# Attention over paired heads: row and column halves of TensorE side by side, scores two pairs ahead, values in parts behind the transposes

## The chip, the cores and the metric

The kernel runs on one core of a Trainium2 chip. The metric is the device time of one execution in microseconds (us); lower is better. Times are the median of several executions.

## The reference, cut to what matters

The program is a network of two blocks over 256 latent tokens (and, in the first block, 256 context tokens) of width 1024. The first block has two layers, each with a feed-forward part, a mixer and a second feed-forward part. The change touches the attention inside the mixer alone. Eight heads of 64 channels; a latent query sees a window of latent keys with a relative bias (others masked) and all 256 context keys; in layer 0 the context tokens also attend to themselves.

```python
def context_attention(q, k, v):
    s = jnp.einsum('bqhd,bkhd->bhqk', q, k, preferred_element_type=jnp.float32) * (NA_HEAD_DIM ** -0.5)
    p = jax.nn.softmax(s, axis=-1).astype(v.dtype)
    return jnp.einsum('bhqk,bkhd->bqhd', p, v).reshape(B, L, NA_CH)

# neighbourhood_attention, per row of the grid
s_loc = einsum(q_r, k_b) * scale + bias
s_ctx = einsum(q_r, k_ctx) * scale
p = softmax(concatenate([s_loc, s_ctx], axis=-1))
o = einsum(p_loc, v_b) + einsum(p_ctx, v_ctx)
```

## The kernel before, in words

Each engine runs its own list of instructions, written out by hand, and waits on counting semaphores. The program is a row of stages. The one of interest is class `Mix`; ahead of it stands `MixIn` (the projection, which fills `u` with queries and keys, channels on the partitions, and `v` with values, tokens on the partitions), behind it `AddProduct` (the output projection, which reads `y`). `Mix` appears once in each layer. In layer 0 it handles two groups: g=0, the latent queries against 512 keys (256 latent, 256 context), and g=1, the context queries against 256 keys. In layer 1 there is only g=0.

An item w is 128 queries (tile `qt`) of one head `h` of one group. There are 8 x 2 items a group. Each passes through this chain:

- **scores** (TensorE, L1267): a product that contracts the 64 channels of a head. Even heads lie on partitions 0 to 63, odd heads on 64 to 127, so the product uses one row half of the array (`po`). It writes 128 x 512 (or 256) into bank w % 2. It waits until VectorE has read item w-2 (`scores_read`).
- **scale** (VectorE, L1367, L1368 and L1371, L1374): scale and bias into `sc`, a ring of four, then the negated row maximum. It waits for the scores, and for the transposes of item w-4, which read the same slot.
- **exps** (ScalarE, L1319): exponential with row sum.
- **normalise** (VectorE, L1382, L1383): reciprocal of the sum, and the product with it.
- **transposes** (TensorE, L1277): one a key tile of 128, four with 512 keys, two with 256, into bank 2 + w % 2.
- **copies** (ScalarE, L1329): from the bank into `pt`, the transposed probabilities.
- **values** (TensorE, L1289): for a whole head (two items), one product a key tile, 128 x 64 weights, 256 columns, summed in one column half of bank 4 or 5.
- **move** (ScalarE, L1337): that half of the bank into `y`, 64 partitions at a time.

TensorE's order is: scores of items 0 to 2; then for each w the scores of w+3, the transposes of w, and on every even w from 2 on the values of the head before. VectorE's order is scale(w+2), normalise(w). ScalarE's is exps(w+2), copies(w), and a move every second item. GpSimd computes the convolution and pooling mixers at the same time (`mixed`); at the end TensorE runs the pooling product (L1307), ScalarE copies it (L1351) and the next stage rounds `y` into operands (L1423, L1435) before its first product (L255).

Of the kernel before, what the change touches and what calls it, by code (L numbers as in the profile page):

```python
# [25 lines left out]
P = 128  # L26
D = 1024
KT = D // P
S = 256
# [21 lines left out]
NA_H, DH = 8, 64  # L51
# [338 lines left out]
A_POOL = A_PT + 2048  # L390
# [802 lines left out]
class Mix:  # L1193
    def __init__(self, chip, layer, last, mix_in):
# [3 lines left out]
        self.sc, self.pt = chip.part(A_SC, 4, 512), chip.part(A_PT, 2, 4, S)  # L1198
# [7 lines left out]
        self.items = [(g, h, qt) for g in range(ng) for h in range(NA_H) for qt in range(2)]  # L1206
# [3 lines left out]
        self.product, self.moved, self.mixed = chip.product.take(n // 2 + 1), chip.moved.take(n // 2), chip.mixed.take(1)  # L1210
        self.y_there = chip.y_there.take(2)

    def keys(self, g):
        return (0, T2) if g == 0 else (S, T2)

# [40 lines left out]
    def tensor(self, pe):  # L1256
# [4 lines left out]
        def scores(w):  # L1261
            g, h, qt = items[w]
            lo, hi = keys(g)
            po, q0 = 64 * (h % 2), g * S + qt * P
            if w >= 2:
                pe.wait_ge(self.scores_read.sem, self.scores_read.at(w - 1))
            nc.tensor.matmul(chip.bank[w % 2][:, 0:hi - lo], u[po:po + 64, CH_Q + h // 2, q0:q0 + P],  # L1267
                             u[po:po + 64, CH_K + h // 2, lo:hi], start=True, stop=True)\
                .then_inc(self.scored.sem, 1)
# [11 lines left out]
        def values(n):  # L1281
            g, h, _ = items[2 * n]
            po = 64 * (h % 2)
            pe.wait_ge(self.copied.sem, self.copied.at(2 * n + 2))
            if n >= 2:
                pe.wait_ge(self.moved.sem, self.moved.at(n - 1))
            nkt = (keys(g)[1] - keys(g)[0]) // P
            for kt in range(nkt):
                mm = nc.tensor.matmul(chip.bank[4 + n % 2][po:po + 64, 0:S],  # L1289
                                      v[:, kt + 4 - nkt, h * DH:(h + 1) * DH], pt[:, n % 2, kt, :],  # L1290
                                      start=(kt == 0), stop=(kt == nkt - 1))
            mm.then_inc(self.product.sem, 1)
# [18 lines left out]
    def scalar(self, act):  # L1311
# [10 lines left out]
        def copies(w):  # L1322
            g, h, qt = items[w]
            nkt = (keys(g)[1] - keys(g)[0]) // P
            n = w // 2
# [3 lines left out]
            nc.scalar.activation(pt[:, n % 2, 0:nkt, qt * P:(qt + 1) * P],  # L1329
                                 chip.bank[2 + w % 2][:, 0:nkt * P].rearrange("p (k q) -> p k q", q=P), ACT.Copy)\  # L1330
                .then_inc(self.copied.sem, 1)

        def move(n):
            g, h, _ = items[2 * n]
            po = 64 * (h % 2)
            act.wait_ge(self.product.sem, self.product.at(n + 1))
            nc.scalar.activation(y[po:po + 64, 4 + h // 2, g * S:(g + 1) * S], chip.bank[4 + n % 2][po:po + 64, 0:S],  # L1337
# [4 lines left out]
        for w in range(len(items)):  # L1342
# [3 lines left out]
            if w >= 3 and w % 2 == 1:  # L1346
                move(w // 2 - 1)
        move(len(items) // 2 - 1)
        act.wait_ge(self.product.sem, self.product.at(len(items) // 2 + 1))
# [4 lines left out]
    def vector(self, dve):  # L1354
# [3 lines left out]
        def scale(w):  # L1358
            g, h, qt = items[w]
            n = keys(g)[1] - keys(g)[0]  # L1360
            s, bank = sc[:, w % 4, :], chip.bank[w % 2]
# [1153 lines left out]
```

## Time and profile before

| | us |
|---|---|
| median of 3 runs | 3099.96 (3099.4 to 3101.96) |
| the profiled execution's own time | 3101.26 |
| its span | 3099.5 |
| TensorE busy (matmul) | 2884.9 (93%) |
| VectorE busy | 2186.3 (71%) |
| ScalarE busy | 1235.7 (40%) |
| `Mix` in layer 0, scores of item 0 to pooling product | 78.9 |
| `Mix` in layer 1, the same | 51.7 |

### The profile page before, as it was taken

Reading aid. Unit: us, or ns where it says so; the run is one execution under the profiler, and the core shown is the slowest. Engines: PE = TensorE matmul, PEld = TensorE weight load, DVE = VectorE, ACT = ScalarE, POOL = GpSimd, SP = SyncE. Lnnn points to the kernel's source line nnn. Section 1 sums busy time; section 2 is a strip of 40 time slices with the busy share of each in tenths; the row PEclk is TensorE's granted clock in tenths of the full one; section 3 lists DMA queues with packets and bytes.
Section 4 is the critical chain, followed back from the end, with each engine's and each line's share of the span. In section 5 each row is a group of like instructions: output and inputs, shape, how many; then the busy total and the mean of one; then the engine's idle time right before and its main releaser. Section 6 shows DMA issues by size and latency. Waiting matters only on the chain. (4 is left out here: it accounts for less than half of the span.)

```text
span 3099.5 us, 46116 instructions
## 1 busy us (share of the span) xinstructions
PE 2884.9 (93%) x15682; PEld 2422.1 (78%) x15682; DVE 2186.3 (71%) x4187; ACT 1235.7 (40%) x2282; POOL 369.4 (12%) x413
## 2 busy tenths in 40 slices
PE   7999999999999999999999997596479999999997
PEld 4888878567888778887859996376368999999997
DVE  2999994559898975657466664365997777777775
ACT  2323243443232332224354453153125555444554
POOL 0111116001111100100400000000473000000000
PEclk9999999999999999999999998798559999999999
DMA  5555443133545444544415556023003655666563
GB/s 233 177 176 203 170 142 102 34 109 136 197 173 194 178 162 143 185 142 148 130 49 170 180 175 216 0 69 109 1 0 96 188 185 187 186 186 188 184 189 115
DMA packets 107703, 449.94 MB, mean 145 GB/s; under 512 B 11952, under 2 KB 12592, under 8 KB 94256
## 3 DMA queue, kind: packets, MB, share of 16 engines
q1 hardware_dynamic: 93744, 347.46, 35.2%
q0 software_dynamic: 13824, 100.67, 8.6%
q8 instruction: 86, 1.41, 0.2%
q14 instruction: 49, 0.40, 0.0%
HBM read 447.04 MB, written 1.05 MB: 145 GB/s over the span
## 5 line engine op out<-in xcount | busy, mean ns | idle before, releaser
L178 DVE TENSOR_TENSOR weight_lo<-weight_ring,weight_hi 128x512 fp32r<-128x512 f32 x1272 | 945.5, 749 | 530.8 <-ACT weight_hi L171 515.8
L171 ACT ACTIVATE weight_hi<-weight_ring 128x512 fp32r<-128x512 f32 x1272 | 800.8, 632 | 1164.4 <-PE bank L257 1163.5
L255 PE MATMUL bank<-operand_hi,weight_hi 128*128 128x256 f32 (+1 forms) x3168 | 1039.4, 328 | 24.0 <-DVE operand_lo L592 13.0
L256 PE MATMUL bank<-operand_lo,weight_hi 128*128 128x256 f32 (+1 forms) x3168 | 1034.7, 327 | 0.0
L257 PE MATMUL bank<-operand_hi,weight_lo 128*128 128x256 f32 (+1 forms) x3168 | 1034.5, 327 | 0.0
L255 PEld LDWEIGHTS bank<-operand_hi,weight_hi 128*128 128x128 f32 x3168 | 603.7, 191 | 91.8 <-issue 21.4
L256 PEld LDWEIGHTS bank<-operand_lo,weight_hi 128*128 128x128 f32 x3168 | 603.9, 191 | 54.6
L257 PEld LDWEIGHTS bank<-operand_hi,weight_lo 128*128 128x128 f32 x3168 | 603.8, 191 | 50.8
L850 DVE SCALAR_TENSOR_TENSOR extension_ffn<-extension_ffn,silu_c 128x512 f32<-128x512 f32 x532 | 388.7, 780 | 1.7
L255 PE MATMUL bank<-hidden_hi_ffn,weight_hi 128*128 128x512 f32 (+1 forms) x704 | 256.6, 364 | 4.0 <-DVE arena L1095 4.0
L256 PE MATMUL bank<-hidden_lo_ffn,weight_hi 128*128 128x512 f32 (+1 forms) x704 | 255.3, 363 | 0.0
L257 PE MATMUL bank<-hidden_hi_ffn,weight_lo 128*128 128x512 f32 (+1 forms) x704 | 255.3, 363 | 0.0
L255 PE MATMUL bank<-weight_hi,act_hi_experts 128*128 128x512 f32 x512 | 201.0, 393 | 1.0 <-DVE act_lo_experts L265 1.0
L256 PE MATMUL bank<-weight_lo,act_hi_experts 128*128 128x512 f32 x512 | 200.7, 392 | 0.0
L257 PE MATMUL bank<-weight_hi,act_lo_experts 128*128 128x512 f32 x512 | 199.2, 389 | 0.0
L255 PEld LDWEIGHTS bank<-hidden_hi_ffn,weight_hi 128*128 128x128 f32 x704 | 132.9, 189 | 28.5 <-DVE arena L1095 6.7
L817 POOL TENSOR_TENSOR mod_lo_ffn<-extension_ffn,mod_hi_ffn 128x1024 fp32r<-128x1024 f32 (+1 forms) x44 | 98.3, 2233 | 427.9 <-ACT mod_hi_ffn L859 427.9
L257 PEld LDWEIGHTS bank<-hidden_hi_ffn,weight_lo 128*128 128x128 f32 x704 | 132.9, 189 | 20.8
L256 PEld LDWEIGHTS bank<-hidden_lo_ffn,weight_hi 128*128 128x128 f32 x704 | 132.9, 189 | 20.5
L801 POOL DMA_DIRECT2D extension_ffn<-in_w_mods x88 | 53.7, 613 | 716.5 <-DVE extension_ffn L850 590.9
L2026 POOL TENSOR_SCALAR arena<-iota,arena 128x128 f32<-128x128 f32 x192 | 125.6, 672 | 78.0 <-ACT arena L2127 78.0
L2142 PE MATMUL bank<-arena 128*128 128x128 f32 x512 | 122.6, 401 | 6.8 <-DVE arena L2038 5.2
(260 smaller groups left out, 2740.1 us busy)
## 6 DMA issues: line engine op xcount, KB each, us to landing
weight_ring<-in_ffn SPq DMA_DIRECT2D x272, 512.0 KB, 3.6
weight_ring<-in_experts SPq DMA_DIRECT2D x256, 512.0 KB, 3.6
extension_ffn<-in_w_mods POOLq DMA_DIRECT2D x96, 1024.0 KB, 7.5
weight_ring<-in_w_mix SPq DMA_DIRECT2D x56, 512.0 KB, 3.6
weight_ring<-in_w_second SPq DMA_DIRECT2D x52, 512.0 KB, 4.0
extension_mixer<-in_rel_bias SPq DMA_DIRECT2D x2, 1536.0 KB, 6.8
arena<-in_x SPq DMA_DIRECT2D x1, 2048.0 KB, 9.4
arena<-in_cmp_k SPq DMA_DIRECT2D x1, 2048.0 KB, 11.8
```

The costliest lines, as they stand in the source:

```text
L171: nc.scalar.activation(self.hi[:, g % 2, h], self.ring[:, g % NS, h], ACT.Copy).then_inc(self.rounded, 1)
L178: self.nc.vector.tensor_tensor(self.lo[:, g % 2, h], self.ring[:, g % NS, h], self.hi[:, g % 2, h].bitcast(F32), ALU.subtract).then_inc(se ...
L255: nc.tensor.matmul(out, a_hi, b_hi, start=start and n == 0, stop=False)
L256: nc.tensor.matmul(out, a_hi, b_lo, start=False, stop=False)
L257: last = nc.tensor.matmul(out, a_lo, b_hi, start=False, stop=stop and n == len(pairs) - 1)
L801: pool.dma_start(self.w[:, j, u, :, :], src).then_inc(self.loaded[j].sem, 16)
L817: nc.gpsimd.tensor_tensor(self.lo[:, 0:n], self.flat(j), self.hi[:, 0:n].bitcast(F32), ALU.subtract)\
L850: ins = nc.vector.scalar_tensor_tensor(acc, w, scale, acc, ALU.mult, ALU.add)
L2026: nc.gpsimd.tensor_scalar(b[:, t % HOTS, :], iota[:, :], columns[:, 1, t:t + 1], None, ALU.is_equal)\
L2142: nc.tensor.matmul(chip.bank[4 + j // 2][:, (j % 2) * P:(j % 2 + 1) * P], a[:, j, :], b[:, j, :], start=True, stop=True).then_inc(chip.spr ...
```

## The change

Heads are handled in pairs. The items of a pair are two neighbouring heads with the same query tile, so that even w is the lower row half and odd w the upper.

- Scores: both products of a pair are issued back to back, into two banks of a ring of four (0, 1, 6, 7 instead of 0, 1). Pair n waits until VectorE has read pair n-2. Pairs 0 and 1 are issued ahead; pair 1 after `MixIn`'s last evictions, since it uses banks 6 and 7. The pair w/2 + 2 is issued before the transposes of even w.
- Values: four items (two heads, two query tiles) make one group n. A part is one key tile: two products back to back, the two heads in the two column halves of one bank. Part w % 4 of group w/4 - 1 follows the transposes of item w, for w from 4 on. The last group's parts stand after the loop.
- `pt` is twice as large (8 x 512 words): [key tile][head of the pair, query]. The copies write it at another place, with the same shape.
- Moves: one for both heads, 128 partitions, half as many; each is issued later.

VectorE's order and instructions stay, but for the bank that scale reads.

```diff
-        self.sc, self.pt = chip.part(A_SC, 4, 512), chip.part(A_PT, 2, 4, S)
+        self.sc, self.pt = chip.part(A_SC, 4, 512), chip.part(A_PT, 8, 4 * P)
...
-        self.items = [(g, h, qt) for g in range(ng) for h in range(NA_H) for qt in range(2)]
+        self.items = [(g, 2 * hp + j, qt) for g in range(ng) for hp in range(NA_H // 2) for qt in range(2) for j in range(2)]
...
+    def score_bank(self, w):
+        return (0, 1, 6, 7)[w % 4]
+
+    def turned_probs(self, n, j, kt):
+
+        return self.pt[:, 4 * (n % 2) + kt, :].rearrange("p (j q) -> p j q", j=2)[:, j, :]
...
+        def scores(n):
+            if n >= 2:
+                pe.wait_ge(self.scores_read.sem, self.scores_read.at(2 * n - 2))
+            for w in (2 * n, 2 * n + 1):
+                g, h, qt = items[w]
+                lo, hi = keys(g)
+                po, q0 = 64 * (h % 2), g * S + qt * P
+                nc.tensor.matmul(chip.bank[self.score_bank(w)][:, 0:hi - lo], u[po:po + 64, CH_Q + h // 2, q0:q0 + P],
+                                 u[po:po + 64, CH_K + h // 2, lo:hi], start=True, stop=True)\
+                    .then_inc(self.scored.sem, 1)
...
+        def values(n, part):
+
+            g, _, _ = items[4 * n]
             nkt = (keys(g)[1] - keys(g)[0]) // P
+            if part >= nkt:
+                return
+            if part == 0:
+                pe.wait_ge(self.copied.sem, self.copied.at(4 * n + 4))
+                if n >= 2:
+                    pe.wait_ge(self.moved.sem, self.moved.at(n - 1))
+            for j in range(2):
+                h = items[4 * n + j][1]
+                mm = nc.tensor.matmul(chip.bank[4 + n % 2][64 * j:64 * j + 64, 0:S],
+                                      v[:, part + 4 - nkt, h * DH:(h + 1) * DH], self.turned_probs(n, j, part),
+                                      start=(part == 0), stop=(part == nkt - 1))
+            if part == nkt - 1:
+                mm.then_inc(self.product.sem, 1)
...
-        for w in range(3):
-            scores(w)
+        scores(0)
         pe.wait_ge(evicted.sem, evicted.at(20))
+        scores(1)
         for w in range(len(items)):
-            if w + 3 < len(items):
-                scores(w + 3)
+            if w % 2 == 0 and w // 2 + 2 < len(items) // 2:
+                scores(w // 2 + 2)
             transposes(w)
-            if w >= 2 and w % 2 == 0:
-                values(w // 2 - 1)
-        values(len(items) // 2 - 1)
+            if w >= 4:
+                values(w // 4 - 1, w % 4)
+        for part in range(4):
+            values(len(items) // 4 - 1, part)
...
-            if w >= 3 and w % 2 == 1:
-                move(w // 2 - 1)
-        move(len(items) // 2 - 1)
+            if w >= 8 and w % 4 == 1:
+                move(w // 4 - 2)
+        move(len(items) // 4 - 2)
+        move(len(items) // 4 - 1)
```

Here is TensorE's order at the start of the stage in layer 0, before. L1267 are scores, L1277 transposes, L1289 values; x4 counts calls in a row.

```order
L1267 MATMUL bank<-extension_mixer 128x512 x4
L1277 MATMUL bank<-ident,extension_mixer 128x128 x4
L1267 MATMUL bank<-extension_mixer 128x512
L1277 MATMUL bank<-ident,extension_mixer 128x128 x4
L1267 MATMUL bank<-extension_mixer 128x512
L1277 MATMUL bank<-ident,extension_mixer 128x128 x4
L1289 MATMUL bank<-extension_mixer 64x256 x4
```

The same place with the change (scores L1275, transposes L1285, values L1301).

```order
L1275 MATMUL bank<-extension_mixer 128x512 x6
L1285 MATMUL bank<-ident,extension_mixer 128x128 x8
L1275 MATMUL bank<-extension_mixer 128x512 x2
L1285 MATMUL bank<-ident,extension_mixer 128x128 x8
L1275 MATMUL bank<-extension_mixer 128x512 x2
L1285 MATMUL bank<-ident,extension_mixer 128x128 x4
L1301 MATMUL bank<-extension_mixer 64x256 x2
L1285 MATMUL bank<-ident,extension_mixer 128x128 x4
L1301 MATMUL bank<-extension_mixer 64x256 x2
```

Six scores stand ahead of the first transposes instead of four, the first values stand behind the fifth item's transposes instead of the third's, and they come two products at a time, one in each column half.

The end of the stage in layer 1, TensorE, before:

```order
L1277 MATMUL bank<-ident,extension_mixer 128x128 x8
L1289 MATMUL bank<-extension_mixer 64x256 x4
L1277 MATMUL bank<-ident,extension_mixer 128x128 x4
L1289 MATMUL bank<-extension_mixer 64x256 x4
L1307 MATMUL bank<-arena,pool_w_pooling 128x256 x2
```

And with the change:

```order
L1285 MATMUL bank<-ident,extension_mixer 128x128 x4
L1301 MATMUL bank<-extension_mixer 64x256 x2
L1285 MATMUL bank<-ident,extension_mixer 128x128 x4
L1301 MATMUL bank<-extension_mixer 64x256 x10
L1321 MATMUL bank<-arena,pool_w_pooling 128x256 x2
```

Behind the last transposes stand ten value products instead of four: one part of the group before, and all four parts of the last group.

## Rows read from the trace of the kernel before

**Rows 1.** Windows: start:end, length, busy of PE, PEld, DVE, ACT, POOL; clock, DMA share, GB/s.

```profile
563.60:570.00 6.40, 4.33 (x10) 1.36 (x10) 5.46 (x13) 6.10 (x12) 0.00 (x0) 0.91 0.21 83
570.00:579.00 9.00, 9.00 (x21) 4.21 (x22) 5.74 (x15) 4.01 (x11) 0.00 (x0) 0.50 0.00 0
579.00:642.60 63.60, 57.20 (x230) 27.54 (x228) 40.28 (x118) 35.38 (x96) 0.00 (x0) 1.00 0.00 1
...
1549.40:1555.50 6.10, 4.18 (x9) 1.24 (x8) 5.21 (x12) 5.85 (x11) 0.00 (x0) 0.98 0.27 86
1555.50:1565.50 10.00, 9.85 (x23) 4.67 (x24) 5.99 (x16) 4.26 (x11) 0.00 (x0) 0.50 0.00 0
1565.50:1601.10 35.60, 32.06 (x131) 15.60 (x129) 20.64 (x54) 18.15 (x40) 0.00 (x0) 1.00 0.00 1
```

**Rows 2.** Timeline, two items with 512 keys: start us, duration us, engine, instruction.

```profile
585.63 1.12 PE L1267 MATMUL bank<-extension_mixer 64*128 64x512 f32 x2
586.69 0.66 PE L1277 MATMUL bank<-ident,extension_mixer 128*128 128x128 f32 x4
...
588.19 0.15 DVE L1382 RECIPROCAL rsum<-rsum 128x1 f32<-128x1 f32 x1
...
588.92 0.66 PE L1277 MATMUL bank<-ident,extension_mixer 128*128 128x128 f32 x4 [0.52 <-DVE extension_mixer L1383]
...
589.50 1.94 PE L1289 MATMUL bank<-extension_mixer 128*64 128x256 f32 x8
...
590.16 0.15 DVE L1382 RECIPROCAL rsum<-rsum 128x1 f32<-128x1 f32 x1
...
591.37 1.12 PE L1267 MATMUL bank<-extension_mixer 64*128 64x512 f32 x2
```

**Rows 3.** Timeline, two items with 256 keys.

```profile
621.18 0.70 PE L1267 MATMUL bank<-extension_mixer 64*128 64x256 f32 x2
621.81 0.44 PE L1277 MATMUL bank<-ident,extension_mixer 128*128 128x128 f32 x2
622.18 0.70 PE L1267 MATMUL bank<-extension_mixer 64*128 64x256 f32 x2
622.71 0.15 DVE L1382 RECIPROCAL rsum<-rsum 128x1 f32<-128x1 f32 x1
...
623.68 1.08 PE L1289 MATMUL bank<-extension_mixer 128*64 128x256 f32 x4
623.96 0.15 DVE L1382 RECIPROCAL rsum<-rsum 128x1 f32<-128x1 f32 x1
...
624.68 0.70 PE L1267 MATMUL bank<-extension_mixer 64*128 64x256 f32 x2
```

**Rows 4.** Timeline, start of the stage in layer 0.

```profile
563.63 1.98 PE L1267 MATMUL bank<-extension_mixer 64*128 64x512 f32 x4
...
569.90 1.11 PE L1277 MATMUL bank<-ident,extension_mixer 128*128 128x128 f32 x4 [1.51 <-DVE extension_mixer L1383]
...
571.33 0.49 DVE L1383 TENSOR_SCALAR extension_mixer<-extension_mixer,rsum 128x512 f32<-128x512 f32 x1
...
573.99 2.07 PE L1267 MATMUL bank<-extension_mixer 64*128 64x512 f32 x2
575.99 1.11 PE L1277 MATMUL bank<-ident,extension_mixer 128*128 128x128 f32 x4
...
577.04 2.93 PE L1289 MATMUL bank<-extension_mixer 128*64 128x256 f32 x8
```

**Rows 5.** Timeline, TensorE at the end of the stage in both layers.

```profile
642.53 1.98 PE L1307 MATMUL bank<-arena,pool_w_pooling 128*128 128x512 f32 x4
...
1597.90 0.66 PE L1277 MATMUL bank<-ident,extension_mixer 128*128 128x128 f32 x4
1599.24 1.94 PE L1289 MATMUL bank<-extension_mixer 128*64 128x256 f32 x8 [0.69 <-ACT extension_mixer L1329]
1601.12 1.13 PE L1307 MATMUL bank<-arena,pool_w_pooling 128*128 128x256 f32 x4
```

More of the change, by code:

```diff
@@ L389 @@
 A_PT = A_SC + 2048
-A_POOL = A_PT + 2048
+A_POOL = A_PT + 4096
 A_MIXER = A_POOL + 2048 - A_WORDS
@@ L1209, in __init__ @@
             s.take(n) for s in (chip.scored, chip.scores_read, chip.maxed, chip.exped, chip.probs, chip.turned, chip.copied))
-        self.product, self.moved, self.mixed = chip.product.take(n // 2 + 1), chip.moved.take(n // 2), chip.mixed.take(1)
+        self.product, self.moved, self.mixed = chip.product.take(n // 4 + 1), chip.moved.take(n // 4), chip.mixed.take(1)
         self.y_there = chip.y_there.take(2)
@@ L1259, in tensor @@
         evicted = self.mix_in.evicted
[L1261 to L1269, printed above, removed]
+        def scores(n):
[8 more added lines that the diff above has]
+                    .then_inc(self.scored.sem, 1)
         def transposes(w):
@@ L1324, in copies @@
             nkt = (keys(g)[1] - keys(g)[0]) // P
-            n = w // 2
+            n = w // 4
             act.wait_ge(self.turned.sem, self.turned.at(w + 1))
@@ L1328, in copies @@
                 act.wait_ge(self.product.sem, self.product.at(n - 1))
-            nc.scalar.activation(pt[:, n % 2, 0:nkt, qt * P:(qt + 1) * P],
+            at = S * (w % 2) + P * qt
+            nc.scalar.activation(pt[:, 4 * (n % 2):4 * (n % 2) + nkt, at:at + P],
                                  chip.bank[2 + w % 2][:, 0:nkt * P].rearrange("p (k q) -> p k q", q=P), ACT.Copy)\
@@ L1333, in move @@
         def move(n):
-            g, h, _ = items[2 * n]
-            po = 64 * (h % 2)
+            g, h, _ = items[4 * n]
             act.wait_ge(self.product.sem, self.product.at(n + 1))
-            nc.scalar.activation(y[po:po + 64, 4 + h // 2, g * S:(g + 1) * S], chip.bank[4 + n % 2][po:po + 64, 0:S],
+            nc.scalar.activation(y[:, 4 + h // 2, g * S:(g + 1) * S], chip.bank[4 + n % 2][:, 0:S],
                                  ACT.Copy).then_inc(self.moved.sem, 1)
@@ L1345, in scalar @@
             copies(w)
-            if w >= 3 and w % 2 == 1:
-                move(w // 2 - 1)
-        move(len(items) // 2 - 1)
-        act.wait_ge(self.product.sem, self.product.at(len(items) // 2 + 1))
+            if w >= 8 and w % 4 == 1:
+                move(w // 4 - 2)
+        move(len(items) // 4 - 2)
+        move(len(items) // 4 - 1)
+        act.wait_ge(self.product.sem, self.product.at(len(items) // 4 + 1))
         for b in range(2):
@@ L1360, in scale @@
             n = keys(g)[1] - keys(g)[0]
-            s, bank = sc[:, w % 4, :], chip.bank[w % 2]
+            s, bank = sc[:, w % 4, :], chip.bank[self.score_bank(w)]
             dve.wait_ge(self.scored.sem, self.scored.at(w + 1))
```

11 lines of the change are left out of this document (removed).

## The prediction

> **What bounds the kernel now.** I read three views of the one profiled execution. First the windows: what does each engine do while the attention stage runs? Then the timeline of TensorE, VectorE and ScalarE inside it, to see which wait ends last. Then the same timeline at the stage's start and end, where the order of work matters most.
>
> The windows [rows 1] show the stage twice: in layer 0 from 563.6 to 642.6 us, in layer 1 from 1549.4 to 1601.1 us, together 131 us of 3100. Neither GpSimd nor the DMA queues do anything that matters there. TensorE is busy 90% of it, VectorE some 60%. In both layers TensorE's clock is at half (1.2 GHz) for 9 to 10 us near the start and at full (2.4 GHz) after that.
>
> The steady stretch of layer 0 [rows 2] repeats every 5.74 us for two items (591.37 - 585.63). Read it as blocks, each from its own start to the next one's. A score product of 512 keys takes 1.06 us (585.63 to 586.69); four transposes take 0.58 (588.92 to 589.50); the values product, eight passes in one column half, takes 1.87 (589.50 to 591.37). 2 x 1.06 + 2 x 0.58 + 1.87 = 5.15. The rest is one wait of 0.52 us for the normalised probabilities [the bracket in rows 2]. So TensorE's own work is the bound, and the wait comes on top. VectorE, where it runs without a wait, needs 1.97 us an item (588.19 to 590.16 between the same instruction), 7.9 for four items, against 11.48 that four items take now: it is the next bound.
>
> With 256 keys [rows 3] the blocks are 0.63 (scores), 0.37 (two transposes) and 1.00 (values, four passes); VectorE needs 1.25 an item; two items take 3.50.
>
> **What changes.** The count of passes, transposes, VectorE and ScalarE instructions per item stays the same (only the moves halve: 12 instead of 24, ScalarE, not on the path). The change alters what stands next to what: two scores back to back in the two row halves and different banks; two value products back to back in the two column halves; scores issued before the wait for probabilities instead of just in time. Three terms follow.
>
> *Term 1, the wait.* Scores of items w+4 and w+5 are out before TensorE waits for item w, so VectorE always has an item to scale. VectorE's loop is then: transposes of w-2 done, scale w+2 (1.4), normalise w (0.6). Worked against TensorE's blocks it is about 1.4 us early each time. The 0.52 per pair goes. If VectorE becomes the bound, it is late next, at 7.9 per four items.
>
> *Term 2, the pairs.* Nothing in this trace has two products in different halves next to each other with long operands, so I bound it. Serial: pair of scores 3 x 0.43 + 0.63 = 1.92, value part (two heads, one key tile) 1.00. Complete overlap: 1.06 and 0.56. Between them: passes start in program order, A1 A2 B1 B2; A2 needs A's half free, B1 needs only B's half and starts beside A2, B2 follows. That hides one pass of four: 1.49 and 0.78. Four items then cost, with 4 x 0.58 for transposes: serial 10.2, staggered 8.4, complete 6.7, where VectorE holds it at 7.9. Now: 11.5. I take staggered, because every row here starts in order and the two halves share no rows (scores) or columns (values). The Trainium skill, TensorE: Matmul & The Clock Gate, Part 3, says that products in different row or column groups run at the same time and that starts and ends keep program order. By its nearly full gain for packed tiles the sum would be the complete case, by its order rule the staggered one.
>
> *Term 3, the edges.* The value parts lag by up to four items, so more of them stand at the end with nothing beside them. Layer 1 ends with four parts after the last transposes.
>
> **The sum, staggered, layer 0.** The first transposes start at 569.90 as before (VectorE decides that). The second wait for the multiply at 571.33, so they run 571.9 to 572.9 [rows 4]. The clock is at half, where scores cost 2.00 for two passes (573.99 to 575.99) and a pair 2.85: 575.8; two transposes 2.1: 577.9; pair: 580.7, where item 4's transposes begin. These and the first value part run cold, 1.1 more than warm, so I count warm from 581.8. Items 4 to 15 take 3 x 8.44, less 3 x 0.64 because the last three pairs of scores have 256 keys: 605.2. Items 16 to 19: 4 x 0.37 + 4 x 0.78 + 2 x 0.85 = 6.3: 611.5. Items 20 to 27: TensorE needs 4.7 per four, VectorE 5.0: 621.5. Up to the last transposes 3.2. Their copy takes 0.9 (layer 1's 1.34 between transposes and values [rows 5], less the shorter transposes and copy), the two value parts 1.2: 626.8. The pooling product started at 642.53 [rows 5]: **-15.7 us**.
>
> *Layer 1* is shifted by 985.8: warm from 1567.6. Items 4 to 11: 3 x 1.49 + 8 x 0.58 + 8 x 0.78 = 15.4: 1583.0. Three items without scores 4.1; last transposes and their copy 1.37 (1.34 today between 1597.90 and 1599.24 [rows 5]); four value parts, nine slots of 0.22 and the edge, 2.1: 1590.6 against 1601.12: **-10.5 us**.
>
> Together -26.2. What follows the pooling product is one chain on ScalarE and VectorE, unchanged. The profiled execution took 3101.26 for a span of 3099.5, 1.3 above the median of 3099.96; it would come to 3075, and from the median I get 3074.
>
> **Rivals.**
> 1. *Serial passes.* The halves don't overlap; only the wait goes. The same walk with 1.92 and 1.00 gives the pooling product at 636.5 and 1597.9: -6.0 and -3.2, so 3091. For it: no row shows an overlap. Against: nothing shared between the halves.
> 2. *Complete overlap, VectorE the bound.* 1.97 an item in layer 0: 623.3 and 1587.5, -19.2 and -13.6, so 3067.
> 3. *Only the scores overlap* (the value products read all 128 partitions for both halves at once). Four items 9.3: about -17, 3083.
> 4. *The clock stays at half.* In both layers it stays low while scores and transposes alternate without a gap, and is back at full only after a block of eight value passes has begun (577.04, with the clock back by 579) [rows 1, 4]. The change puts the first values two transposes later and cuts them into parts of four passes between transposes. Cold, four items cost 2 x 2.85 + 4 x 1.05 + 4 x 1.45 = 15.7 instead of 8.4. If it holds for the whole stage, the walk ends at 661 and 1609: 18.7 and 8 later, 3127. Each four items at half take back 7.3, so the gain is gone after about 3.6 such groups, some 55 us. Against it: the full clock has held through the 0.52 us waits of today [rows 1, 2], and TensorE's blocks would be closer together. The Trainium skill, TensorE: Matmul & The Clock Gate, Part 4, says that transposes don't count as busy for the clock, which speaks for this rival; no row here separates transposes from the rest.
>
> The opposite of 4 is a bonus, not a rival: six scores instead of four before the first transposes may keep the clock up. Item 4 would then start at 577.8, VectorE's pace, some 4 us earlier in each layer.
>
> **Chances.** Staggered 0.46, complete 0.16, serial 0.20, scores only 0.09, clock 0.06, something that cancels it 0.03. A measurement of this kernel can tell about 0.2%, 6.2 us, from no change. The serial case is faster by 9, with prices uncertain by some 3 us, so a little of it falls inside. Faster 0.88, within 0.05, slower 0.07. The range runs from the complete case, or the staggered one with the clock kept up (3066 to 3067), to the serial case: 3065 to 3092. It leaves out mostly rival 4.
>
> **What would show it.** In the changed profile, the starts inside a pair of scores tell term 2: 0.43, 0, 0.43 apart is staggered; 0.43 three times is serial; all within 0.45 is complete. Four items with 512 keys should take 8.4 us, with no wait of TensorE for the probabilities; a wait there, with VectorE busy throughout, means complete. The windows should show half clock for about 13 us and not later. The pooling product should begin near 627 and 1591. I am wrong if the four items take over 10.5 us, or if the gap from pooling product to the next stage (4.8 us in layer 0) grows.

## The result and the profile after

| | before | changed |
|---|---|---|
| median, us | 3099.91 (3099.4 to 3101.96, 4 runs) | 3063.32 (3061.79 to 3070.09, 4 runs) |
| ratio, 95% interval | | 0.9883 [0.9867, 0.9898] |
| profiled execution, us | 3101.26, span 3099.5 | 3061.79, span 3060.0 |
| stage, layer 0, us | 78.90 (563.63 to 642.53) | 55.83 (562.56 to 618.39) |
| stage, layer 1, us | 51.74 (1549.38 to 1601.12) | 37.49 (1525.21 to 1562.70) |

Here and below a stage runs from the first score product to the pooling product. The kernel is 36.6 us faster by the medians. The forecast was 26 faster, and the result lies 1.7 us below the range. The two profiled executions differ by 39.5 us; the two stages account for 37.3 of it (23.1 and 14.2). The rest is small: 1.1 us before the first stage and 1.1 behind the second, in work that the change doesn't touch. One later execution of the changed kernel took 5098.65 us at a mean granted clock of 0.723 and is left out of its median in the table below.

The page of the changed kernel, busy time by engine:

```profile
PE 2834.0 (93%) x15682; PEld 2395.6 (78%) x15682; DVE 2183.9 (71%) x4187; ACT 1227.3 (40%) x2270; POOL 368.0 (12%) x413
```

Its windows over the same stretches as [rows 1], with the same columns:

```profile
562.50:570.00 7.50, 3.83 (x17) 1.35 (x16) 6.50 (x15) 6.68 (x13) 0.00 (x0) 1.00 0.21 71
570.00:579.00 9.00, 5.63 (x31) 2.78 (x32) 8.68 (x25) 6.58 (x15) 0.00 (x0) 1.00 0.00 1
579.00:618.40 39.40, 34.24 (x213) 15.51 (x211) 35.14 (x107) 28.41 (x82) 0.00 (x0) 1.00 0.00 1
...
1525.20:1535.00 9.80, 5.34 (x25) 2.07 (x24) 8.75 (x22) 8.40 (x17) 0.00 (x0) 1.00 0.20 54
1535.00:1562.70 27.70, 22.10 (x138) 10.52 (x136) 22.44 (x60) 18.41 (x41) 0.00 (x0) 1.00 0.00 1
```

Two things changed. From 570 to 579 us TensorE was busy for all nine microseconds at half clock [rows 1]; now it is busy for 5.63 at full clock (in this execution: e11 below shows another). And VectorE, busy 63% of the steady stretch before (40.28 of 63.60), is busy 89% of it now (35.14 of 39.40), slightly more than TensorE.

The timeline of two items with 512 keys, after, against [rows 2]:

```profile
583.82 1.13 PE L1275 MATMUL bank<-extension_mixer 64*128 64x512 f32 x4
583.89 0.15 DVE L1397 RECIPROCAL rsum<-rsum 128x1 f32<-128x1 f32 x1
...
584.88 0.66 PE L1285 MATMUL bank<-ident,extension_mixer 128*128 128x128 f32 x4
...
585.87 0.15 DVE L1397 RECIPROCAL rsum<-rsum 128x1 f32<-128x1 f32 x1
...
586.60 0.66 PE L1285 MATMUL bank<-ident,extension_mixer 128*128 128x128 f32 x4 [0.48 <-DVE extension_mixer L1398]
...
587.19 0.65 PE L1301 MATMUL bank<-extension_mixer 128*64 128x256 f32 x4
587.77 1.13 PE L1275 MATMUL bank<-extension_mixer 64*128 64x512 f32 x4
```

Read it in three steps.
- The first row is a pair of scores: four passes whose block, to the next row's start, takes 1.06 us (583.82 to 584.88). Two passes took 1.06 before. So one product of the pair costs nothing.
- A value part of four passes takes 0.58 (587.19 to 587.77).
- Two items now take 3.95 us (583.82 to 587.77), thus 7.90 for four against 11.48. TensorE's blocks are 2 x 1.06 + 4 x 0.58 + 4 x 0.58 = 6.76 of that; the rest is the wait in the bracket, once per two items. VectorE runs at 1.98 us an item (583.89 to 585.87) without a pause. The wait is there because VectorE can't go faster.

To see when the passes of a pair start, I cut the timeline off 0.1 us behind the pair's start: it then holds those passes alone that have begun.

```profile
583.82 0.70 PE L1275 MATMUL bank<-extension_mixer 64*128 64x512 f32 x2
```

Two passes start together. Cut off at 584.3 the row still counts two, at 584.4 all four: the other two follow together, half a microsecond behind. Below, a *slot* is the time that one pass takes.

TensorE at the start of the stage, against [rows 4]. It waits for VectorE's probabilities before each of the first transposes. They begin at 568.82, 570.80, 572.77, 574.75 and 576.72 (items 0 to 4), so VectorE's 1.98 us an item sets the pace from the first item on:

```profile
568.82 0.65 PE L1285 MATMUL bank<-ident,extension_mixer 128*128 128x128 f32 x4 [1.54 <-DVE extension_mixer L1398]
...
570.80 0.65 PE L1285 MATMUL bank<-ident,extension_mixer 128*128 128x128 f32 x4 [1.32 <-DVE extension_mixer L1398]
```

And at the end of the stage in both layers, against [rows 5]:

```profile
618.39 1.98 PE L1321 MATMUL bank<-arena,pool_w_pooling 128*128 128x512 f32 x4
...
1559.48 0.66 PE L1285 MATMUL bank<-ident,extension_mixer 128*128 128x128 f32 x4
1560.07 2.70 PE L1301 MATMUL bank<-extension_mixer 128*64 128x256 f32 x20
1562.70 1.13 PE L1321 MATMUL bank<-arena,pool_w_pooling 128*128 128x256 f32 x4
```

### The profile page after: what moved, and what is told of

It reads as the page before. It is cut to its first block and busy times, and to the rows that moved or that the text cites. A ratio compares the mean times of both kernels' runs of the same rounds, so it can differ in the third digit from the quotient of the medians.

```text
span 3060.0 us, 46082 instructions
## 1 busy us (share of the span) xinstructions
PE 2834.0 (93%) x15682; PEld 2395.6 (78%) x15682; DVE 2183.9 (71%) x4187; ACT 1227.3 (40%) x2270; POOL 368.0 (12%) x413
## 5 line engine op out<-in xcount | busy, mean ns | idle before, releaser
L255 PE MATMUL bank<-operand_hi,weight_hi 128*128 128x256 f32 (+1 forms) x3168 | 1039.4, 328 | 24.0 <-DVE operand_lo L592 12.9
```

What stands on the lines that cost most here:

```text
L255: nc.tensor.matmul(out, a_hi, b_hi, start=start and n == 0, stop=False)
```

## The experiments

The question was what made the stage 37 us shorter: products beside each other, the order, or the clock. All kernels start from the changed one, except e4. Stage lengths are of the profiled execution.

| | median, us (number of runs) | ratio to before, 95% | stage, layer 0 / 1, us | four items, us |
|---|---|---|---|---|
| before | 3099.91, 3101.31, 3099.72, 3098.36 in four sets | | 78.90 / 51.74 | 11.48 |
| changed | 3063.32 (4) | 0.9883 [0.9867, 0.9898] | 55.83 / 37.49 | 7.90 |
| e1, scores of a pair in one half | 3081.76 (4) | 0.9939 [0.9922, 0.9955] | 59.96 / 46.35 | 8.5 |
| e2, values of a part in one half | 3071.07 (4) | 0.9900 [0.9883, 0.9917] | 61.38 / 40.35 | 8.5 |
| e3, both | 3090.28 (5) | 0.9966 [0.9951, 0.9980] | 72.27 / 47.60 | 10.2 |
| e4, before, with small products as filler | 3093.83 (9) | 0.9974 [0.9964, 0.9985] | 75.66 / 48.15 | |
| e5, gap behind the stage filled | 3066.15 (4) | 0.9893 [0.9877, 0.9910] | 55.83 / 37.68 | |
| e6, ScalarE scales half of the scores | 3064.72 (4) | 0.9889 [0.9873, 0.9906] | 56.11 / 37.98 | 7.3 |
| e7, values in one block | 3063.82 (4) | 0.9888 [0.9872, 0.9905] | 57.22 / 37.90 | |
| e8, scores one pair ahead | 3129.60 (4) | 1.0099 [1.0082, 1.0115] | 95.5 / 62.2 | 12.9 |
| e9, values in one block, head after head | 3072.57 (2) | 0.9913 [0.9893, 0.9933] | 58.47 / 42.72 | |
| e10, e6, e5 and filler at the start | 3060.40 (4) | 0.9875 [0.9858, 0.9891] | 57.70 / 36.29 | |
| e11, the changed kernel again | 3064.97 (3) | 0.9890 [0.9870, 0.9910] | 57.91 / 37.81 | |

The changed kernel stands against the first set of before, e1 to e4 against the second, e5 to e8 against the third, e9 to e11 against the fourth.

### e1: the two scores of a pair in the same row half

Neighbours in the list of items become the two query tiles of one head, so a pair uses one row half; bank, count and lead stay.

```
-        self.items = [... for qt in range(2) for j in range(2)]
+        self.items = [... for j in range(2) for qt in range(2)]
...
-                h = items[4 * n + j][1]
+                h = items[4 * n + 2 * j][1]
...
-            at = S * (w % 2) + P * qt
+            at = S * (h % 2) + P * qt
```

> The two scores of a pair are now the two query tiles of one head, so both use the same row half; all else as in the changed kernel. Theory (overlap of halves, VectorE bound): the four score passes start 0.43 us apart, a pair costs 1.92 instead of 1.06 us, four items 2 x 1.92 + 4 x 0.58 + 4 x 0.58 = 8.5 us instead of the 7.9 that VectorE needs. Some 4 us slower than the changed kernel (3067). Rival (the halves count for nothing, the order of issue does it all): four items stay at 7.9 and the time at 3063. On the clock: if it is the fuller array that keeps TensorE at the full clock at the start of the stage, it falls again here for about 10 us in each layer, 3 to 5 us more in each (3072 to 3077); if it is the two more scores ahead of the first transposes, it stays full.

The timeline of TensorE in e1, scores of two pairs in a row:

```profile
579.86 1.98 PE L1275 MATMUL bank<-extension_mixer 64*128 64x512 f32 x4
...
584.11 1.98 PE L1275 MATMUL bank<-extension_mixer 64*128 64x512 f32 x4
```

Four passes in one half take 1.98 instead of 1.13, and two items 4.25: 8.5 for four. TensorE's blocks give the same, 2 x 1.92 + 4 x 0.58 + 4 x 0.58 = 8.5. So it is the other half that makes a score free, and without it TensorE is the bound again. Layer 0's stage is 4.1 us longer for it. Layer 1's is 8.9 us longer, which takes the time (3081.76) beyond all that was expected, and its windows say why:

```profile
1540.00:1545.00 5.00, 5.00 (x13) 2.45 (x12) 3.91 (x11) 2.48 (x6) 0.00 (x0) 0.50 0.00 0
...
1550.00:1555.00 5.00, 5.00 (x10) 1.70 (x11) 2.08 (x6) 1.30 (x3) 0.00 (x0) 0.50 0.00 0
```

Fifteen microseconds at half clock, with TensorE busy in all of them. The same program ran at 1.00 from 570 to 579 us in layer 0 (0.57 in the four microseconds before). So what the pairs put into the array does not by itself settle the clock.

### e2: the two value products of a part in the same column half

Part by part, the passes of one head for two key tiles stand together, then those of the other head.

```
-            for j in range(2):
+            for m in (2 * part, 2 * part + 1):
+                j, kt = m // nkt, m % nkt
...
-                                      v[:, part + 4 - nkt, ...], self.turned_probs(n, j, part),
-                                      start=(part == 0), stop=(part == nkt - 1))
+                                      v[:, kt + 4 - nkt, ...], self.turned_probs(n, j, kt),
+                                      start=(kt == 0), stop=(kt == nkt - 1))
```

> A part of the values is now one head with two key tiles, so both products use the same column half; all else as in the changed kernel. With 256 keys the first part is the first head, the second part the other. Theory: the four passes start 0.22 us apart, a part costs 1.00 instead of 0.58 us, four items 2 x 1.06 + 4 x 0.58 + 4 x 1.00 = 8.4 us with 512 keys, and the four parts at the end of layer 1 take 3.7 instead of 2.6 us. About 5 to 7 us slower than the changed kernel (3069). Rival (value products don't gain from column halves, the 0.58 has another cause such as the new place of the probabilities): unchanged, 3063. The clock should stay full at the stage's start in both, since the values come late there.

TensorE's timeline in e2:

```profile
581.12 1.13 PE L1275 MATMUL bank<-extension_mixer 64*128 64x512 f32 x4
...
582.76 1.08 PE L1302 MATMUL bank<-extension_mixer 128*64 128x256 f32 x4
...
585.36 1.13 PE L1275 MATMUL bank<-extension_mixer 64*128 64x512 f32 x4
```

The scores still take 1.13, and a value part takes 1.08 instead of 0.65. Two items take 4.24: 8.5 for four; the blocks give 2 x 1.06 + 4 x 0.58 + 4 x 1.00 = 8.4. Rival 3, that only the scores overlap, is out: the value products overlap too, though both halves read all 128 partitions at once.

### e3: both

The edits of e1 and e2 together. What is left of the change is the order, the longer lead and the fewer moves.

> Both of the above: only the order of issue and the single move are left of the change. Theory: four items 10.2 us, TensorE the bound without a wait for the probabilities. From the walk of the serial case 3091 with the clock at half at the start, 3083 with it full. Rival (order of issue is what matters, since it takes the waits away): below 3075. If it is the fuller array that holds the clock, half clock shows here at the stage's start.

TensorE's timeline in e3, and windows of its start:

```profile
587.07 1.98 PE L1275 MATMUL bank<-extension_mixer 64*128 64x512 f32 x4
...
592.17 1.98 PE L1275 MATMUL bank<-extension_mixer 64*128 64x512 f32 x4
```

```profile
573.00:576.00 3.00, 3.00 (x4) 0.96 (x4) 2.79 (x8) 1.20 (x3) 0.00 (x0) 0.50 0.00 0
...
582.00:585.00 3.00, 3.00 (x9) 1.46 (x8) 1.60 (x5) 1.30 (x3) 0.00 (x0) 0.50 0.00 0
585.00:588.00 3.00, 3.00 (x11) 1.66 (x11) 2.09 (x6) 1.30 (x3) 0.00 (x0) 0.84 0.00 0
```

Two items take 5.10, 10.2 for four, which is the serial figure of term 2. The half clock is back too, from 573 to 585 us. The time, 3090.3, is that of rival 1 (3091). So the walk was right about a kernel whose passes don't overlap, clock included, and most of the error is in the overlap.

The four kernels before, e3, e1 or e2, and changed, also split the gain. The order alone gives 11.0 us (3101.3 to 3090.3). The scores side by side give 19.2 more (3090.3 to 3071.1), the values side by side 8.5 more (3090.3 to 3081.8), both together 27.0 (to 3063.3). Each share includes what the clock did in those executions, and the kernels are of different sets, whose medians of before differ by up to 3 us.

### e4: the kernel before, with its clock kept up

Small 128-column products, whose result nobody reads, stand ahead of the transposes that TensorE waits for at the start of the stage.

```
+            if w >= 1:
+                chip.keep_warm(pe, 3, 2)
...
+            if w == 0:
+                chip.keep_warm(pe, 3, 6)
```

> The kernel before, with small full-array products of constants in TensorE's gaps at the start of the stage: two each after the second and third item's scores, six ahead of the first transposes (about 2 us of work, in a bank that nobody reads yet). Theory (the gaps and the thin work of half-row scores let the clock fall): the clock stays at 2.4 GHz from 570 to 579 us, the first items take some 4 us less in each layer, 3092. Rival (the clock falls for what comes after, transposes and single scores in turn): half clock shows as before and the time is 3100 to 3101.

Windows of e4 where before ran at 0.50 [rows 1]:

```profile
570.00:573.00 3.00, 2.93 (x11) 1.01 (x8) 2.64 (x8) 2.06 (x5) 0.00 (x0) 1.00 0.00 0
...
576.00:579.00 3.00, 2.67 (x8) 0.91 (x8) 1.86 (x5) 1.28 (x3) 0.00 (x0) 1.00 0.00 0
```

The clock stays at full, the stages get 3.2 and 3.6 us shorter, and the kernel 7.5. The stages' 6.8 us are the price of the half clock in the kernel before, measured by itself and net of what the filler costs. The bonus of the prediction put it at 4 us a layer.

### e5: the gap behind the stage

The changed kernel shows half clock in a place that the prediction didn't look at, behind the pooling product's wait, in both layers:

```profile
623.20:627.60 4.40, 4.39 (x12) 3.47 (x13) 4.07 (x7) 4.27 (x8) 0.03 (x1) 0.61 0.00 0
...
1565.80:1569.60 3.80, 3.80 (x19) 3.80 (x20) 2.16 (x7) 2.99 (x7) 0.00 (x0) 0.55 0.00 0
```

e5 puts small products there:

```
+        chip.keep_warm(pe, 2, 11 if self.ng == 2 else 7)
```

> The changed kernel, with 11 (layer 0) and 7 (layer 1) small full-array products of constants behind the pooling product, where TensorE waits 2.8 and 1.9 us for the next stage's operands. In the changed kernel the clock is at half from about 624 to 627.5 us and from 1566 to 1569.6 us, behind these gaps. Theory (the gap lets the clock fall): the next stage starts at the full clock, about 1.7 us less in each layer, 3 us in all (3060). Rival (the fall comes from what ran before the gap, or the gap is too short to matter): half clock as before, 3063.

The same places in e5:

```profile
623.50:628.00 4.50, 4.47 (x20) 3.71 (x21) 4.09 (x7) 4.29 (x8) 0.11 (x1) 1.00 0.02 4
...
1564.70:1569.00 4.30, 4.29 (x36) 4.30 (x37) 2.89 (x8) 3.57 (x9) 0.00 (x0) 1.00 0.01 4
```

The clock is at full, and the kernel at 3066.15 is not to be told from the changed one (3063.32, and 3064.97 in e11). Whatever full clock brings there is smaller than the spread of the runs. The profiles show it for layer 0: from its pooling product to layer 1's first score it is 905.26 us in e5 against 906.82 in the changed kernel, 1.6 less, near the 1.7 expected. Behind layer 1 nothing is gained (1497.47 and 1497.30 us to the end of the span).

### e6: a part of VectorE's work on ScalarE

If VectorE is the bound, taking an instruction from it must shorten the items. e6 scales the 256 context columns of the scores on ScalarE, three items ahead.

```
+            nc.scalar.activation(sc[:, w % 4, S:T2], chip.bank[self.score_bank(w)][:, S:T2], ACT.Copy, scale=0.125)\
+                .then_inc(self.context_scaled.sem, 1)
...
-                nc.vector.tensor_scalar(s[:, S:T2], bank[:, S:T2], 0.125, None, ALU.mult)\
```

> The changed kernel, with the scaling of the 256 context scores (VectorE, 0.41 us an item with 512 keys) moved to ScalarE, three items ahead. Theory (VectorE sets the pace at 1.97 us an item): VectorE needs about 1.6, ScalarE about 1.7 and TensorE 1.68 an item, so four items take some 7.0 us instead of 7.9: 24 items at 0.2 less give 5 us, 3058. Rival (another loop, such as probabilities to transposes to copies, sets the 7.9): four items stay at 7.9, 3063.

TensorE's timeline in e6 over four items, and its start by windows:

```profile
581.98 1.13 PE L1278 MATMUL bank<-extension_mixer 64*128 64x512 f32 x4
...
589.30 1.13 PE L1278 MATMUL bank<-extension_mixer 64*128 64x512 f32 x4
```

```profile
570.00:575.00 5.00, 3.91 (x12) 1.94 (x12) 3.96 (x10) 3.97 (x10) 0.00 (x0) 0.52 0.01 2
575.00:580.00 5.00, 4.18 (x20) 2.30 (x20) 3.86 (x10) 3.19 (x10) 0.00 (x0) 0.80 0.00 2
```

Four items take 7.32 instead of 7.90: VectorE was the bound. The start of the stage gave it back, at a granted clock of 0.52 and 0.80 where the changed kernel's profile shows 1.00. Not all of that is the clock: the first transposes begin 7.5 us behind the first score (563.04 to 570.57) instead of 6.3, because VectorE's first instruction now waits for ScalarE's scaling (1.64 us), and ScalarE has other work at that time. The total didn't move.

### e7: the value parts as one block

```
-            if w >= 4:
-                values(w // 4 - 1, w % 4)
+            if w >= 4 and w % 4 == 0:
+                for part in range(4):
+                    values(w // 4 - 1, part)
```

> The changed kernel, with the four parts of a group's values issued together behind the transposes of its following item instead of one part behind each item's transposes. Same work, halves still side by side. Theory (VectorE bound with some 1.4 us to spare on TensorE's side): the block of 16 passes takes 2.1 us at one place, the transposes behind it come late by less than what VectorE has to spare, within 3 us of the changed kernel (3063 to 3066). Rival (the cut into parts is what keeps VectorE fed): four items take 8.5 us or more, 3068 or more.

The block of 16 passes, the halves taking turns, in e7:

```profile
585.21 1.95 PE L1301 MATMUL bank<-extension_mixer 128*64 128x256 f32 x16
```

16 passes take 1.95 us where eight of one half took 1.94 before [rows 2]. The time is 3063.82. So cutting the values into parts, one key tile behind each transpose, brings nothing that can be measured here.

### e8: scores one pair ahead instead of two

```
-            if w % 2 == 0 and w // 2 + 2 < len(items) // 2:
-                scores(w // 2 + 2)
+            if w > 0 and w % 2 == 0 and w // 2 + 1 < len(items) // 2:
+                scores(w // 2 + 1)
```

> The changed kernel, with the scores issued one pair ahead: pair w/2 + 1 before the transposes of even w, so that VectorE must scale item w+2 right after its scores and before it normalises item w. Theory (issuing two pairs ahead is what takes the wait out): in each pair TensorE waits from the scores' end for scale and normalise, about 2 us, while VectorE has waited for the scores; two items take 1.06 + 2.0 + 2 x 1.17 = 5.4 us instead of 3.95, some 1.5 us for each of 20 pairs, 3090. Rival (the overlap alone brings the gain, the distance does not matter): 3063 to 3067.

TensorE and VectorE over two items of e8:

```profile
596.16 1.13 PE L1275 MATMUL bank<-extension_mixer 64*128 64x512 f32 x4
...
597.32 0.42 DVE L1382 SCALAR_TENSOR_TENSOR extension_mixer<-bank,extension_mixer 128x256 f32<-128x256 f32 x1 [2.99 <-PE bank L1275]
...
599.44 0.66 PE L1285 MATMUL bank<-ident,extension_mixer 128*128 128x128 f32 x4 [2.15 <-DVE extension_mixer L1398]
...
602.59 1.13 PE L1275 MATMUL bank<-extension_mixer 64*128 64x512 f32 x4
```

The pair is still side by side, yet the kernel is 29.9 us slower than before. VectorE waits 2.99 us for scores, then TensorE waits 2.15 for the probabilities that come of them; two items take 6.43 at full clock (5.4 expected), and much of the stage runs at half (0.78 on average from 563 to 690 us). So the 29.9 us are the lost lead and the lower clock together; four items at full clock, 12.9 us against 11.48 before, leave the clock out. The merged kernel with one pair ahead has lost the order that kept both engines busy. The lead of two pairs is what turns the overlap into time.

### e9: the block of values, head after head

e7 again, but all eight passes of one half first and then the eight of the other.

```
-                for part in range(4):
-                    values(w // 4 - 1, part)
+                values(w // 4 - 1)
...
+            for j in range(2):
+                for part in range(nkt):
```

> e7 (the values of a group in one block of 16 passes) with another order inside the block: all four key tiles of the even head, then all four of the odd head, instead of the two heads in turn. In e7 the block takes 1.95 us. Theory (a pass may only run beside one in the other half that stands next to it in the order, since passes start in order): one pass at the border is hidden, the block takes 15 x 0.22 + 0.1 = 3.4 us. Rival (the halves are separate queues and later passes overtake): 1.95 us as before. Time of the kernel by the theory 3064 to 3070, by the rival 3064.

The block of a group with 512 keys in e9 whole, and then as it stands when the view is cut off at 595.5, 595.8, 596.4 and 597.0 us. Each row counts the passes that have begun by then:

```profile
594.82 2.86 PE L1298 MATMUL bank<-extension_mixer 128*64 128x256 f32 x16
```

```profile
594.82 0.86 PE L1298 MATMUL bank<-extension_mixer 128*64 128x256 f32 x3
...
594.82 1.35 PE L1298 MATMUL bank<-extension_mixer 128*64 128x256 f32 x6
...
594.82 1.94 PE L1298 MATMUL bank<-extension_mixer 128*64 128x256 f32 x11
...
594.82 2.43 PE L1298 MATMUL bank<-extension_mixer 128*64 128x256 f32 x14
```

Sixteen passes one after the other would take 16 x 0.22 = 3.5 us, eight pairs 1.9 (e7). Starts strictly in program order would hide one pass, 3.3. Measured is 2.79 to the next block: some 12 slots, so four passes are hidden. By the counts the first and the last starts come singly, one per slot, and those between, from 595.5 to 596.4, two per slot (eight in 0.9 us). Passes of the second half run ahead of waiting ones of the first, but only a few deep. Groups with 256 keys have four passes of one half first and then four of the other, and they show how deep:

```profile
607.86 1.09 PE L1298 MATMUL bank<-extension_mixer 128*64 128x256 f32 x8
```

The kernel's time, 3072.57 us, is above the 3064 to 3070 expected. Layer 1's stage is the longer one (42.72 against 37.90 in e7); one of its blocks ran at half clock, 4.52 us for 16 passes.

### e10: the fastest version, and e11: the changed kernel again

e10 is e6 and e5, with filler ahead of the first two transposes:

```
+            if w < 2:
+                chip.keep_warm(pe, 3, 5 - 2 * w)
```

> The changed kernel with e6 (ScalarE scales the context scores) and e5 (the gap behind the pooling product filled), and small products of constants ahead of the first two transposes (5 and 3). Theory: e6's steady gain (7.3 instead of 7.9 us for four items with 512 keys, 6 groups, 3.5 us) was given back by the half clock that came at the start of the stage; filled, it stays, and the next stage starts at the full clock (3 us): 3057. Rival (the runs scatter by more than that, and what is left of either is lost elsewhere): 3063.

> The changed kernel as it is, in the same job as e10, to have both against the same runs: 3063, between 3061 and 3070 as before.

Windows of e10, then of e11 at the start of layer 0's stage and in layer 1's:

```profile
562.00:570.00 8.00, 5.63 (x20) 2.40 (x20) 4.90 (x11) 7.28 (x16) 0.00 (x0) 0.81 0.22 66
570.00:579.00 9.00, 6.95 (x43) 4.13 (x42) 7.26 (x19) 6.80 (x18) 0.00 (x0) 0.98 0.01 2
...
1536.00:1562.20 26.20, 22.73 (x141) 10.52 (x137) 19.80 (x51) 20.88 (x53) 0.00 (x0) 1.00 0.01 2
```

```profile
570.00:579.00 9.00, 7.16 (x32) 3.28 (x32) 8.62 (x23) 5.69 (x14) 0.00 (x0) 0.81 0.00 1
...
1539.00:1566.90 27.90, 24.67 (x138) 11.59 (x136) 22.44 (x60) 17.77 (x41) 0.00 (x0) 0.89 0.00 1
```

e10 takes 3060.40 us, its four runs 3059.45 to 3061.58, against 3057 expected. Its clock held in layer 1, where VectorE is busy 19.80 of 26.20 us and the stage is 1.2 us shorter than the changed kernel's. In layer 0 it held from 570 to 579 us only (0.81 before that, 0.94 from 579 to 619.7), and the stage is no shorter (57.70 against 55.83 and 57.91). The seven runs of the changed kernel, here and above, lie between 3061.79 and 3070.09, all above e10's highest. The intervals of the ratios overlap, so the gain of 3 to 5 us over the changed kernel is likely rather than shown.

e11 shows where the changed kernel's spread comes from, at least in part: the same program ran 570 to 579 us at 0.81 of the full clock here and at 1.00 in the first profile, and its stage in layer 0 is 2.1 us longer. Over the seven runs the mean granted clock goes down, by and large, as the time goes up, from 0.959 at 3061.79 us to 0.954 at 3070.09. In layer 1, whose items all have 512 keys, the lower clock hardly costs anything: at 0.89 TensorE is busy 24.67 us instead of 22.10, but VectorE 22.44 as before, and the stage is 0.3 us longer. TensorE has time to spare once VectorE is the bound.

## Why the prediction was wrong

The sign, the bound and the mechanism held: the time fell because products in different halves run beside each other. The size was 37 us and not 26, outside the range. By the steps:

- *What bounds the kernel.* Right. TensorE's blocks made up the time before, and VectorE's 1.97 us per item came next; it is 1.98 now.
- *Term 1, the wait.* As far as it is a term by itself, e3 shows it: the order without any overlap gives 11.0 us, where rival 1's walk gave 9. The wait is gone there. e8 shows the other side, what the lead is worth (12.9 us for four items with one pair less in advance, where the changed kernel takes 7.90).
- *Term 2, the pairs.* This step failed: **"passes start in program order, A1 A2 B1 B2"**. It gave 1.49 for a pair of scores and 0.78 for a value part; measured are 1.06 and 0.58, the complete case (1.06 and 0.56). Two passes start together at the pair's beginning, not one. I had taken that order "because every row here starts in order", and that overlooked rows of the kernel before, which stand below this list. e9 is the direct test: four passes of 16 are hidden and four of eight, where program order hides one. The Trainium skill, TensorE: Matmul & The Clock Gate, Part 3, says that products in different row or column groups run at the same time, and the trace agrees for both kinds. It also says that starts keep program order; e9's do not, and the measurement decides. (The changed kernel's pairs alone would leave it open, if the order is that of products and not of passes.)
- *The bound that follows.* Four items 8.4 predicted, 7.90 measured, with a wait of TensorE for the probabilities and VectorE busy throughout. That is what the prediction named as the mark of the complete case, and e6 confirms VectorE as the bound (7.32 with less work on it).
- *Term 3 and the clock.* The sum counted the start of each stage at half clock until 581.8; its profile shows 1.00 throughout. The prediction named this as a bonus and gave it no place in the sum. e3 shows half clock again when nothing overlaps, e4 what it costs in the kernel before (3.2 and 3.6 us in the stages). In the changed kernel it is not a fixed property: e11's profile has some of it in both layers.
- *Rivals.* The serial case is e3: predicted 3091, measured 3090.3. The values overlap too (e2 against the changed kernel), so rival 3 is out. Rival 4, clock at half for the whole stage, did not come in the changed kernel, but a version of it appears in e1's layer 1 and in e8. The Trainium skill, TensorE: Matmul & The Clock Gate, Part 4, says that transposes don't count as busy for the clock, which spoke for rival 4. It was not tested apart: no run here separates transposes from the products around them.

The rows that were overlooked: the kernel before has 16 products of 64 rows and 15 columns, in another stage, whose row halves alternate (L1750). Cut off at 1998.6 and at 1998.8 us, their row counts two passes and four, where the order of the prediction would start with one:

```profile
1998.49 0.40 PE L1750 MATMUL bank<-arena 64*128 64x15 f32 x2 [0.42 <-ACT arena L1773]
...
1998.49 0.61 PE L1750 MATMUL bank<-arena 64*128 64x15 f32 x4 [0.42 <-ACT arena L1773]
```

Their operands are short, so they could not give the price of 512 columns, but they spoke for the complete case, which got a chance of 0.16.

In the profiled execution the miss adds up so. The two stages were to lose 26.2 us and lost 37.3. The complete case with VectorE as the bound was worked out at 32.8, so choosing the staggered one cost 6.6. The other 4.5 I put down to the clock. This is an estimate, no run isolates it: item 4 would begin at 577.8 by VectorE's pace, where the walk with complete pairs at half clock has it at 580.1 (579.0, and 1.1 for the cold work behind it), 2.3 in each layer. This adds up in the sum, less well in each layer: 19.2 + 2.3 = 21.5 against 23.1 measured in layer 0, 13.6 + 2.3 = 15.9 against 14.2 in layer 1. The start is not what is off: item 4's transposes begin 14.16 us behind the first score in both layers, as reckoned (563.63 to 577.8). From there to the pooling product it is 41.67 us in layer 0 (43.2 in the walk) and 23.33 in layer 1 (21.6 in the walk).

The range failed for another reason than the centre. It took the complete overlap and the clock kept up each by itself (3066 to 3067), as alternatives. They came together in the first profile. They may not be independent: among the kernels with a lead of two pairs, those that lack the overlap (e3, and e1 in layer 1) are the ones whose clock stays low longest. That is argued from one profile of each, not shown. Both together would have put the low end near 3062.

**What stays open.** What decides whether the clock falls at the start of the stage: the changed kernel's own executions differ (1.00 and 0.81 from 570 to 579 us), e1 had it low for up to 4 us at the start of layer 0 and for 15 and more in layer 1, e4's filler held it in both layers, and e10's held it only in part. The runs show which executions kept it, not the rule. And which pass overtakes which inside a block, as said at e9.

## What to carry to other kernels

Products of 64 rows or 64 columns in different halves of the array, next to each other in the program, were worth their full overlap here (two for the time of one), and this held for both directions; price such a pair first by the complete case, then look for the engine that becomes the bound. Before taking an order of starts for granted, look through the whole trace for products of the same kind, also in stages that the change leaves alone. The overlap only turns into time if the next engine has work in stock: the same pairs with one pair less in advance made the kernel 30 us slower than before. And when two effects can come together, as overlap and clock did, the range must hold them together, not each alone.

## What was unexpected of the hardware

- Two-pass fp32 products in different halves start in pairs, and a pair of 64-row, 512-column products takes 1.06 us where one takes 1.06 and two in the same half 1.92. Two value products in two column halves take 0.58 instead of 1.00.
- Passes of one half overtake waiting ones of the other, some three deep: 16 passes take 1.95 us alternating (e7) and 2.79 with one half's eight first (e9), by estimate 3.5 one after the other; eight passes take 1.08 alternating and 1.09 with one half's four first.
- More TensorE activity in time did not mean more clock. Up to 570 us TensorE was busy 4.33 of 6.40 us in the kernel before, and the clock fell (0.91, then 0.50); in the changed kernel it was busy 3.83 of 7.50, and the clock stayed at 1.00. In e1's layer 1 TensorE was busy without a gap for 15 us at 0.50. (Busy times at half clock are long because the clock is low, so 9.00 of 9.00 at 0.50 and 5.63 of 9.00 at 1.00 do not compare as work.)
- Half clock can be nearly free where TensorE is not the bound: at 0.89 instead of 1.00 over layer 1's steady part, the changed kernel's stage was 0.3 us longer (e11). In layer 0 it was 2.1 us longer, at 0.81 and 0.94.
- The granted clock at one place differs between executions of one program (1.00 and 0.81), which is part of this kernel's spread of 8 us.
